# Paired scores and alternating values in the attention heads of the second block

## The reference

```python
# branch A: 4 heads, two softmaxes c = 0, 1 over 64 dimensions each, values of 128
s = einsum('bqhcd,bkhcd->cbhqk', qi, k) * scale + bias        # causal
p = softmax(where(mask, s, NEG_INF));  w = p[0] - lam * p[1]
oa = einsum('bhqk,bkhe->bqhe', w, v)
# branch B: 8 heads in 2 groups (64 dimensions), window of 128 keys, a sink in the softmax
# branch C: 8 heads in 2 groups; per head three softmaxes, gated and summed:
out = g[..., 0:1] * o_cmp + g[..., 1:2] * o_sel + g[..., 2:3] * o_win
#   cmp: 31 compressed keys; sel and win: here all keys up to the query's own
# behind them, per token and branch
gate = sigmoid(mg);   x = x + sum(gate * y) @ w_out
```

## Time and profile before

| | us |
|---|---|
| median of 3 runs (4089.55 to 4106.05) | 4097.31 |
| the profiled execution, as timed | 4107.89 |
| its span in the trace | 4105.8 |
| first score to last value matmul of the stage heads, start 3115.7 to end 3591.2 | 475.5 |
| TensorE busy over the whole span | 3850.4 (94%) |
| VectorE busy | 1879.8 (46%) |
| ScalarE busy | 993.8 (24%) |

### The profile page before, as it was taken

How to read it: one execution, slowest core, us unless ns; L and a number is a source line. 1 busy time by engine, 2 the same in 40 slices (tenths; PEclk the granted TensorE clock), 3 DMA queues, 4 the chain that set the end, 5 groups by cost and what they waited for, 6 DMA issues and landing times. The chain is left out here.

```text
span 4105.8 us, 51266 instructions
## 1 busy us (share of the span) xinstructions
PE 3850.4 (94%) x19583; PEld 3048.2 (74%) x19583; DVE 1879.8 (46%) x2689; ACT 993.8 (24%) x1744; POOL 1965.1 (48%) x834
## 2 busy tenths in 40 slices
PE   7999999999988998899999999899799999999999
PEld 4777788888877887676678888777585555577877
DVE  3444335645548883344426656466214444463200
ACT  3333112222210001333312222100214544412200
POOL 2433342332335554344453443688443333387886
PEclk9999999999999999999999999999899999999999
DMA  6211221211226543222232221344422222253333
GB/s 211 49 44 48 77 48 42 53 40 42 53 66 123 118 99 111 67 57 58 60 79 58 54 62 49 92 92 129 128 53 72 65 55 66 63 159 77 97 88 92
DMA packets 485311, 317.84 MB, mean 77 GB/s; under 512 B 38185, under 2 KB 456370, under 8 KB 483210
## 3 DMA queue, kind: packets, MB, share of 16 engines
q1 hardware_dynamic: 466080, 288.59, 28.6%
q10 hardware_dynamic: 19050, 26.75, 1.9%
HBM read 282.71 MB, written 32.56 MB: 77 GB/s over the span
## 5 line engine op out<-in xcount | busy, mean ns | idle before, releaser
L938 POOL TENSOR_TENSOR whi<-ring,con 128x1024 fp32r<-128x1024 f32 (+1 forms) x415 | 978.7, 2358 | 2085.7 <-DMA ring<-in_w_in 1597.8
L615 PE MATMUL ps<-xT_parts,whi 128*128 128x512 f32 (+2 forms) x2632 | 1019.1, 387 | 71.0 <-DVE zz L2225 18.3
L615 PE MATMUL ps<-hT_parts,whi 128*128 128x512 f32 (+1 forms) x2864 | 1050.4, 367 | 0.0
L940 POOL TENSOR_TENSOR ring_parts<-ring,whi 128x1024 fp32r<-128x1024 f32 (+1 forms) x415 | 989.4, 2384 | 32.5
L615 PE MATMUL ps<-xT_parts,ring_parts 128*128 128x512 f32 (+2 forms) x2600 | 946.8, 364 | 0.0
L615 PE MATMUL ps<-arena_parts,whi 128*128 128x512 f32 (+1 forms) x2344 | 726.0, 377 | 53.7 <-DVE arena_parts L2257 36.1
L1651 ACT ACTIVATE arena<-ps 128x768 f32<-128x768 f32 (+9 forms) x561 | 298.6, 542 | 1638.4 <-PE ps L615 786.2
L615 PE MATMUL ps<-arena 128*128 128x128 f32 (+9 forms) x3292 | 642.2, 338 | 11.9 <-DVE arena L2225 9.0
L615 PEld LDWEIGHTS ps<-xT_parts,whi 128*128 128x128 f32 (+1 forms) x2632 | 501.6, 191 | 177.5 <-issue 87.8
L615 PEld LDWEIGHTS ps<-hT_parts,whi 128*128 128x128 f32 x2864 | 544.9, 190 | 89.9 <-issue 7.2
L615 PEld LDWEIGHTS ps<-arena 128*128 128x128 f32 (+3 forms) x3292 | 433.9, 192 | 166.9 <-issue 130.3
(11 more groups left out here) (173 smaller groups left out, 3644.2 us busy)
## 6 DMA issues: line engine op xcount, KB each, us to landing
ring<-in_w_in SPq DMA_DIRECT2D x504, 256.0 KB, 4.1
arena<-in_w_ada SPq DMA_DIRECT2D x64, 256.0 KB, 5.9
ring<-in_w_up SPq DMA_DIRECT2D x64, 256.0 KB, 4.0
ring<-in_w_down SPq DMA_DIRECT2D x64, 256.0 KB, 3.9
ring<-in_w_out SPq DMA_DIRECT2D x48, 256.0 KB, 3.9
gates_kept<-stage ACTq DMA_DIRECT2D x24, 384.0 KB, 4.1
arena<-gates_kept SPq DMA_DIRECT2D x24, 384.0 KB, 3.8
arena<-in_w_ada SPq DMA_DIRECT2D x8, 1024.0 KB, 19.7
```

The source lines that it names most:

```text
L615: return nc.tensor.matmul(o, l, r, start=first, stop=last)
L938: v.tensor_tensor(hi, raw, ones[:, 0:m].unsqueeze(1).to_broadcast([P, kt, m]), ALU.mult).then_inc(w_rounded, 1)
L940: v.tensor_tensor(ringR[:, s, 0:kt, 0:m], raw, hi.bitcast(F32), ALU.subtract).then_inc(w_split, 1)
```

## The change

Six things are changed in the stage heads:

1. **Order of the units.** For B, sel and win the two groups of a `qt` follow one another (group 0, group 1), where all of group 0 came before. With A's c0 and c1 that makes neighbours 2k, 2k + 1 of equal width whose operands lie on the two halves of the array's rows. cmp stays one group after the other, with both neighbours on the same half.
2. **Scores in pairs.** `scores(n)` issues the matmuls of n and n + 1 back to back, and TensorE's step n issues `scores(n + 2)` at even n, where every step issued `scores(n + 3)`.
3. **Values.** B, sel and win take both groups in turn, matmul by matmul, on the lower and upper 64 columns; cmp's values come by themselves. Six value blocks a pass (`PV`) where there were five.
4. **Where the transposed probabilities lie.** Two uses share an area of five rows (`pT_at`), the second running backwards. Same copies, other addresses.
5. **VectorE's order.** `normalise(n)`, then `maximum(n + 2)`.
6. **A gate tile ahead.** Gate tile 0 is loaded ahead of the bias rows, computed between `gates_turned` and the first scores, and goes through ScalarE ahead of `exp(0)`. 35 tiles are left for the fill, and `unit_us` has new costs (three half-pairs' worth of scores at even n, none at odd n).

```diff
-            for kind, g, subs in (("A", 0, ("c",)), ("B", 0, ("b",)), ("B", 1, ("b",)),
-                                  ("C", 0, ("sel", "win", "cmp")), ("C", 1, ("sel", "win", "cmp"))):
...
+            for kind, sub, groups in (("A", "c", (0,)), ("B", "b", (0, 1)), ("C", "sel", (0, 1)), ("C", "win", (0, 1)),
+                                      ("C", "cmp", (0,)), ("C", "cmp", (1,))):
+                for qt in range(LT):
...
-        VALUES_AT = [("A", 0, 8, 2), ("B", 0, 17, 2), ("B", 1, 19, 2), ("C", 0, 28, 3), ("C", 1, 40, 3)]
+        VALUES_AT = [("A", 8, 2), ("B", 17, 2), ("sel", 25, 2), ("win", 33, 2), ("cmp0", 36, 1), ("cmp1", 41, 1)]
...
-        FILL_TILES, gates_planned = [], 0
+        FILL_TILES, gates_planned = [], 1
...
-            if n + 3 < 4 * NS2:
-                total += 2 * (heads2[n + 3]["w"] / 1200 + 0.1)
+            if n % 2 == 0 and n + 2 < 4 * NS2:
+                total += 3 * (heads2[n + 2]["w"] / 1200 + 0.1)
...
+                    load_gate(0)
...
-                mm(b, q, k, True, True).then_inc(scores2, 1)
+                return score_bank(n, u["w"]), q, k
+
+            def scores(n):
+
+                for b, q, k in [operands(n + c) for c in range(2)]:
+                    mm(b, q, k, True, True).then_inc(scores2, 1)
...
+                elif kind in ("sel", "win"):
+                    for s in range(LT):
+                        for g in range(2):
+                            todo.append((bank(1)[rows[g], s * P:], (vS if kind == "sel" else vW)[:, s, rows[g]],
+                                         pT_keys(use[g], s, s * P, LAT - s * P), kind == "sel" and s == 0, False))
...
-                        pe.wait_ge(gate2_tanh, before.count("gate"))
+                        pe.wait_ge(gate2_tanh, 1 + before.count("gate"))
...
+            pe.wait_ge(w_split, splits.number() + 1)
+            for k in range(KT):
+                fill_step(k)
             pe.wait_ge(n2_ready, NORM0 + 4)
-            for n in range(3):
-                scores(n)
+            scores(0)
...
-                if n + 3 < 4 * NS2:
-                    scores(n + 3)
+                if n % 2 == 0 and n + 2 < 4 * NS2:
+                    scores(n + 2)
...
+            product()
+            do(gate_out2[0], bank(2).rearrange("p (a n) -> p a n", a=2), ACT.Tanh, scale=0.5).then_inc(gate2_tanh, 1)
+            tiles.next()
             exp(0)
             exp(1)
...
+                normalise(n)
                 if n + 2 < 4 * NS2:
                     maximum(n + 2)
-                normalise(n)
```

More of the change, by code:

```diff
@@ L413, in two_blocks @@
         assert used[0] <= more
-        pT2 = take(3 * LT, LAT, at=KT * ALL)
+        assert KT * ALL + 10 * LAT <= base
         rawA, sqA, rsA = stage[:, 0:LAT], zz[:, 0, 0:LAT], zz[:, 1, 0:LAT]
@@ L563, in unit_us @@
             total = 0.0
-            if n + 3 < 4 * NS2:
-                total += 2 * (heads2[n + 3]["w"] / 1200 + 0.1)
+            if n % 2 == 0 and n + 2 < 4 * NS2:
+                total += 3 * (heads2[n + 2]["w"] / 1200 + 0.1)
             if n < 4 * NS2 and heads2[n]["sub"] != "c0":
                 total += 0.1 + 0.11 * -(-heads2[n]["w"] // P)
-            for kind, g, first, per in VALUES_AT:
+            for kind, first, steps in VALUES_AT:
                 j, o = divmod(n - first, NS2)
-                if 0 <= j < 4 and o < (2 if kind != "C" else 3):
-                    total += {"A": 1.1, "B": 0.9, "C": 1.3 if o == 2 else 2.2}[kind]
+                if 0 <= j < 4 and o < steps:
+                    total += {"A": 1.1, "B": 1.0, "sel": 1.3, "win": 1.3}.get(kind, 0.9)
             return total
@@ L1533, in turn, with values @@
                 last.then_inc(turned2, 1)
[L1535 to L1539, removed]
+            def values(i, kind, step, steps):
+                mine = [u for u in heads2 if u["i"] == i and
+                        (u["kind"] == kind or u["sub"] == kind or u["sub"] + str(u["g"]) == kind)]
+                use = {u["g"]: u["use"] for u in mine}
+                rows = [slice(g * 64, g * 64 + 64) for g in range(2)]
@@ L1560, in values @@
-                for args in sum(steps[step * per:(step + 1) * per], []):
+                        for s in range(max(t - 1, 0), t + 1):
+                            for g in range(2):
+                                todo.append((bank(1)[rows[g], t * P:(t + 1) * P], vB[:, s, rows[g]],
+                                             pT_keys(use[g], s, t * P, P), s == max(t - 1, 0), s == t))
+                elif kind in ("sel", "win"):
+                    for s in range(LT):
+                        for g in range(2):
+                            todo.append((bank(1)[rows[g], s * P:], (vS if kind == "sel" else vW)[:, s, rows[g]],
+                                         pT_keys(use[g], s, s * P, LAT - s * P), kind == "sel" and s == 0, False))
+                else:
+                    g = int(kind[-1])
+                    todo.append((bank(1)[rows[g], :], vc[0:NB2, g], pTcmp[0:NB2], False, True))
@@ L1561, in values @@
+                per = -(-len(todo) // steps)
+                for args in todo[step * per:(step + 1) * per]:
                     last = mm(*args)
-                if (step + 1) * per >= len(steps):
+                if step + 1 == steps:
                     last.then_inc(pv2, 1)
```

73 lines of the change are left out of this document (36 added, 37 removed).

## The result

| | before | after |
|---|---|---|
| median, 8 runs each | 4100.38 us (4089.55 to 4106.05) | 4129.5 us (4118.43 to 4136.47) |
| ratio, 95% interval | 1 | 1.0070 (1.0058 to 1.0082) |
| span of the profiled run | 4105.8 us | 4134.6 us |
| TensorE busy over the span | 3850.4 us | 3807.9 us |
| the stage heads (as below) | 478.2 us | 503.3 us |

The change makes the kernel 0.7% slower, although TensorE is busy for 43 us less. The forecast was 4132. All rows come from one execution of each kernel; that of the changed one is the slowest of its eight (4136.47 us), with a granted clock of 0.959 where the seven others had 0.962 or 0.963.

The account below looks back on a forecast made before the run. The prediction took the stage to be TensorE's queue (busy 458.7 of 475.6 us). 74.6 us less work, 82 more of waits and 28 more for the clock made +35 us: median 4132 us, range 4065 to 4185.

Parts of the forecast that it names:

- scores: TensorE's score matmuls, issued in pairs on the array's two row halves, take 63.3 us instead of 112.0: 48.7 us less.
- values: B's and C's value matmuls, alternating between the array's column halves, take half of their 46.1 us: 23 us less.
- idle ahead of the first score: TensorE's 2.86 us wait for VectorE before the first score is filled by the gate tile ahead: 3 us less.
- (a): At query tile ends, TensorE's mean-square matmul waits for Square and Copy behind the exponential of a just-issued score: 25 us more.
- (b): At gate tile ends, TensorE waits for the Tanh, which stands behind an exponential and sometimes a table load: 41 us more.
- (d): The tile behind a query tile waits for Ln behind a table load, 1 to 2 us at 9 places: 8 us more.
- (c): Odd turns wait for a normalise that VectorE does behind the maximum of a recently issued score: 8 us more.
- clock: Some 30 long waits, two in three followed by a stretch at 0.50 costing 1.4 us: 28 us more, bounds 0 and 55.
- TensorE remains the bound: Faster rival: waits grow by 45 us and the clock by 5, so -25 us: 4072 us; chance 0.20.
- Even: Rival: waits as computed but the clock no worse, or a smaller part of both: 4104 us; chance 0.25.

Follow-up runs that it names:

- act_first: The changed kernel with Tanh, Square and Copy moved ahead of the exponential on ScalarE, TensorE's order untouched: 4058.07 us, ratio 0.9890 to the kernel before.
- pair_early: The changed kernel with each pair of scores issued one turn earlier, in the odd step behind its turn: 4042.05 us, ratio 0.9851 to the kernel before.
- norm_pair: The changed kernel with VectorE going by pairs, two normalise and then two maximum in place of one each in turn: 4105.92 us, ratio 1.0024 to before.
- split: The changed kernel with the score pairs of B and C taken apart, the second score behind the step's turn: 4135.49 us, ratio 1.0100 to before.
- val_group: The changed kernel with value matmuls of group 0 ahead of group 1 within each step's share, no longer alternating: 4121.89 us, ratio 1.0062 to before.
- val_steps: The changed kernel with the value matmuls of the two groups in steps of their own: 4150.67 us, ratio 1.0113 to the kernel before.

## Why the prediction was right, and where it was not

| step | predicted, us | measured, us |
|---|---|---|
| scores | -48.7 | -44.7 |
| values | -23 | -24.6 |
| idle ahead of the first score | -2.9 | -2.9, 1.2 of it back at the first turn |
| (a) mean-square matmuls | +25 (30 from 5.9) | +17 (21.0 from 4.4) |
| (b) gate tiles and (d) the tile behind a query tile | +49 (62 from 13) | +40 (47.2 from 7.5) |
| (c) turns | +8 (12 from 4) | +18 (21.7 from 3.9) |
| clock | +28 | +27.0 |
| sum | +35 | +25.1 in the stage, +28.8 in the span |

(The transposes' rows give 5.3 us less work and the rest 1.6 more; together with scores and values that is the -73.0 above.)

- **Scores.** The overlap is as forecast; both sizes were a little off. Before, by the starts of successive rows at full clock, a score cost no 0.10 us beyond its own pace (98.1 us in all, not 112.0). Now a pair costs what one score cost, 1.06 for 512 and 0.42 for 128, where I had left a second fixed part in it (53.4 in all, not 63.3): the second score starts 6 or 7 ns behind the first, not 50; the 4 ns that the prediction sets beside its own reading were nearer. The two errors cancel but for 4 us.
- **(a) and (b)** hold as a mechanism, shown by act_first and pair_early, which remove them by different edits. The sizes are too high at every place: in a pass (a) waits 2.63, 1.77, 1.32 and 1.28 us, where I had 3, 2.6 to 3.1, 1.9 and 2.1 (10.1 in sum, measured 7.0), and (b) 1.65, 2.91, 3.18, 1.31 and 1.75, where I had 2.0, 3.2, 3.4, 1.6 and 2.0. The chain of the first place is 3134.00 - 3130.24 = 3.76 us; I had added up 4.0, of which 0.86 was the exponential with the reading of its sum; Square begins 0.67 us behind the exponential's start, beside that reading. In the last pass (b) has 8.9 us at the seven boundaries, and not 13.7. Why the other places of (a) and the last pass are further off I have not worked out.
- **(c)** is the term that was too small, 21.7 for 12. norm_pair shows that the order is its cause. I had no price for one thing: 13.1 of these us are at 11 turns shortly behind an operation of VectorE on 128x1 that took 0.8 to 2.3 us (the median of its kind is 0.16). The last section shows what it ends with. It was in the kernel before too and lay beside other work.
- **(d)** is too high: 5.9 us at seven places, not 12 at nine, and 2.7 of them are put down to a weight split on GpSimd.
- **Clock.** 22 stretches at 0.50, 86.3 us, against 7 and 30.7. That 28 and 27.0 agree is luck. The forecast had some 30 long waits, two in three with a stretch of 1.4 us of loss behind it; there were 42 over 1.2 us, about one stretch for two of them, and a stretch cost 41.2/22 = 1.9 us (in the kernel before already 14.2/7 = 2.0). The waits of before that it counted from were misread too: the one of 1.9 us lies ahead of the stage, and the five in it that had a stretch near their end are 1.1 to 1.7 us, beside the 2.86 ahead of the first score. Over the table, kernels with 13 to 42 such waits have about half as many stretches (16 for 23 in split is the most), the one with 10 has 7, and those with 0 to 5 have 1 to 7. That the stretches fall with the waits over the fourteen kernels is as far as the runs go; no run changed the clock alone, so that the waits cause them is likely and not shown.
- **The rivals.** "TensorE remains the bound" was to be decided at the mean-square matmul: 1.5 us or 3. It waits 2.63. "Even" did not come, although the waits were 8 us below my sum, because the clock was not better than I said. The stage ends at 3617, not before 3571, idle 91 and not under 60.

The direction and the mechanism were right; that the net is nearer than its parts is luck: the waits are 8 too high in sum, with (c) 10 too low inside, and the work is 1 off with errors of opposite sign.

## What to carry to other kernels

Before two small matmuls are put side by side, ask when the chain that starts at them must have come back: here the same pair of instructions was worth +0.7% or -1.5% by standing one turn later or earlier. On the engine that reads the results, put the instruction whose input is long there (the Tanh of an ended tile) ahead of the one whose input was only just asked for. Look at the granted clock beside the waits: in the changed kernel 71 us more of idle time came with 27 us more lost at the lower clock.

## What the runs showed of the hardware that I had not expected

**A pair for the price of one.** 512-wide scores: 1.06 us for two on the two halves of the rows, 1.05 for one. At half clock I had read 0.37 us of fixed time into the stage's first four pairs; at full clock the same eight instructions take 3120.98 - 3120.13 = 0.85 us, where the earlier trace rows had 1.65.

```profile
3120.13 0.93 PE L624 MATMUL ps<-arena 64*128 64x128 f32 x8
3120.98 0.49 PE L624 MATMUL ps<-xT_parts,whi 128*128 128x512 f32 x1
```

**The halves need not alternate.** In val_group matmuls on the second half of the columns seem to have started beside those of the first, though three others of the first half stood between them in the program. A record doesn't say which half it is; I infer it from the widths, as only two records of 512 belong to each half, and from the time, 1.66 us as with alternating halves. val_steps, where the halves can't meet, has 2.30 us for each group's 512, 384, 256 and 128. By the Trainium skill, "TensorE: Matmul & The Clock Gate", section "Step-by-step: what each phase is for", matmuls stay in program order and only weight loads are pulled ahead. The starts in this run differ from that: the later group's first matmul begins 14 ns behind the earlier group's first. The measurement decides here, as far as the inference from the widths goes; what makes it possible no run tells.

**VectorE stands still for a pass of GpSimd.** At 3298.02 in the changed kernel a turn waits 2.31 us for VectorE. GpSimd, VectorE and TensorE there:

```profile
3294.89 2.34 POOL L948 TENSOR_TENSOR whi<-ring,con 128x1024 fp32r<-128x1024 f32 x1 [9.51 <-DMA ring<-in_w_in]
```

```profile
3295.58 1.66 DVE L2839 TENSOR_TENSOR small<-small 128x1 f32<-128x1 f32 x1
...
3297.48 0.48 DVE L2845 TENSOR_SCALAR arena<-ps,small 128x256 f32<-128x256 f32 x1
```

```profile
3298.02 0.44 PE L1547 MATMUL ps<-con,arena 128*128 128x128 f32 x2 [2.31 <-DVE arena L2845]
```

The addition, one number per row, ends at 3297.24, and GpSimd's pass at 3297.23. In the stage 22 of the 80 such small operations of VectorE with two inputs take over 0.5 us, and each of the 22 ends within 0.03 us of the end of a GpSimd pass (21 of 21 in the kernel before); beyond their own 0.16 us they hold VectorE for 29 us. The reciprocal, as small and with one input, is not held: 28 of its 160 start inside a GpSimd pass, and none takes over 0.17 us. The Trainium skill, "SBUF — State Buffer", section "SBUF: two separate sides", calls the pair of ports that these two engines share an exclusive lock: of a VectorE operation with two inputs in SBUF and a GpSimd operation that reads SBUF, the one that starts first has it for the whole instruction, and the other is blocked. The trace agrees: the 22 start inside the pass (2.34 us here) with whose end they end. No run changed the operation to one with a single input, so what it would give back was not measured.
